# Two expert layers with a token mixer between them: gathered expert rows against both tables streamed through TensorE

## The reference, cut to what matters

```python
def peer_block(xb, w_q, sub_keys, expert_u, expert_v):
    q = (xb @ w_q).reshape(T, PEER_HEADS, 2, PEER_HALF)      # 8 heads
    s = einsum('thpd,hpkd->thpk', q, sub_keys)               # 2 x 128 keys
    sv, si = top_k(s, 16)
    cand = sv[:, :, 0, :, None] + sv[:, :, 1, None, :]
    cidx = si[:, :, 0, :, None] * 128 + si[:, :, 1, None, :]
    top_s, pos = top_k(cand, 16)
    eidx = take_along_axis(cidx, pos)                        # 16 experts a head
    gate = softmax(top_s)
    act = gelu(einsum('thkd,td->thk', expert_u[eidx], xb))
    return einsum('thk,thkd->td', gate * act, expert_v[eidx])
```

## Time and profile before

| | |
|---|---|
| time, median of 3 runs | 3167.44 us (3167.44 to 3170.0) |
| span of the profiled execution | 3165.3 us |
| TensorE busy | 2588.5 us (82%) |
| VectorE busy | 2022.9 us (64%) |
| ScalarE busy | 1229.5 us (39%) |
| bytes moved by DMA | 1179.94 MB, mean 373 GB/s |
| the indirect queue's packets | 82.1% of 16 DMA engines' span |

### The profile page before, as it was taken

One profiled execution on the slowest core, in us unless ns is written; L12 is line 12 of the kernel. 1 busy time (PEld: TensorE's weight loads), 2 busy tenths in 40 slices (PEclk: granted clock), 3 DMA queues, 4 the chain that ended last, 5 costly groups with the idle time before them and its releaser, 6 DMA issues.

```text
span 3165.3 us, 35978 instructions
## 1 busy us (share of the span) xinstructions
PE 2588.5 (82%) x12092; PEld 1064.0 (34%) x12092; DVE 2022.9 (64%) x5008; ACT 1229.5 (39%) x3892; POOL 1074.3 (34%) x1041
## 2 busy tenths in 40 slices
PE   7999998878777877778988878888777877978777
PEld 3555653323222323223333344333223332322111
DVE  4533457777777777665555757667777776765544
ACT  3122335443443444334323533444344543443323
POOL 0000014433433444333433334343443443343331
PEclk9999999899999989999999999999999999999999
DMA  9411359999999999999999999999999999999995
GB/s 353 155 54 53 125 204 405 421 421 418 415 420 421 419 408 414 418 417 411 418 415 417 416 411 393 416 419 421 420 418 417 416 419 416 405 420 422 418 421 243
DMA packets 198780, 1179.94 MB, mean 373 GB/s; under 512 B 20994, under 2 KB 21700, under 8 KB 67268
## 3 DMA queue, kind: packets, MB, share of 16 engines
q0 software_dynamic: 147456, 1073.81, 82.1%
q1 hardware_dynamic: 51140, 103.84, 8.9%
HBM read 1175.48 MB, written 2.10 MB: 372 GB/s over the span
## 4 chain that ended last, share of the span: by engine, by line
DMA 47%; PE 14%; ACT 5%; DVE 4%; issue 3%; POOL 3%; DVEq 0%; POOLq 0%
DMA ring<-in_expert_rows,idx_v 18%; DMA ring<-in_peer_rows,idx_v 11%; DMA scr<-in_expert_rows,idx_v 9%; DMA scr<-in_peer_rows,idx_v 8%; PE banks L1166 8%; PE banks L814 6%; DVE ring L2299 2%; POOL ring L788 1%; DVE scr L2299 1%; DMA scr<-in_w_in 1%; POOL scr L788 1%; ACT ring L1688 1%; ACT L1682 1%; ACT scr L1682 1%; ACT L1644 1%
## 5 line engine op out<-in xcount | busy, mean ns | idle before, releaser
L1166 PE MATMUL banks<-ring 128*32 128x512 f32 x2016 | 809.5, 621 | 251.7 <-ACT ring L1688 241.4
L1166 PE MATMUL banks<-scr,ring 128*32 128x512 f32 x2080 | 819.8, 613 | 215.5 <-ACT ring L1688 214.8
L1682 ACT ACTIVATE scr<-scr 128x1 f32<-128x1 f32 x1024 | 206.9, 202 | 1511.9 <-DVE scr L2299 1510.4
L2299 DVE CUSTOM_DVE_ANT_0 scr<-scr,ring 128x1024 f32<-128x1024 f32 x390 | 478.0, 1226 | 305.9 <-DMA scr<-in_peer_rows,idx_v 157.4
L2299 DVE CUSTOM_DVE_ANT_0 ring<-ring 128x1024 f32<-128x1024 f32 x378 | 463.1, 1225 | 302.0 <-DMA ring<-in_expert_rows,idx_v 166.7
L788 POOL DMA_INDIRECT scr<-in_peer_rows,idx_v x264 | 272.7, 1033 | 475.9 <-PE banks L1166 355.7
L814 PE MATMUL banks<-hT,scr 128*128 128x128 f32 (+3 forms) x2576 | 367.7, 303 | 66.4 <-DVE ring L2281 47.3
L1166 PEld LDWEIGHTS banks<-ring 128*32 128x32 f32 x2016 | 162.8, 111 | 770.2 <-ACT ring L1688 486.8
L788 POOL DMA_INDIRECT ring<-in_expert_rows,idx_v x256 | 271.1, 1059 | 422.1 <-PE banks L1166 389.3
L1166 PEld LDWEIGHTS banks<-scr,ring 128*32 128x32 f32 x2080 | 165.9, 111 | 737.3 <-ACT ring L1688 458.4
L788 POOL DMA_INDIRECT ring<-in_peer_rows,idx_v x248 | 263.1, 1061 | 409.4 <-PE banks L1166 371.0
(11 more groups left out here) (255 smaller groups left out, 2247.4 us busy)
## 6 DMA issues: line engine op xcount, KB each, us to landing
scr<-in_w_in SPq DMA_DIRECT2D x8, 2048.0 KB, 28.4
scr<-in_w_mod SPq DMA_DIRECT2D x7, 2048.0 KB, 12.8
ring<-in_w_in SPq DMA_DIRECT2D x7, 2048.0 KB, 12.8
scr<-in_w_q SPq DMA_DIRECT2D x6, 2048.0 KB, 27.8
ring<-in_w_mod SPq DMA_DIRECT2D x5, 2048.0 KB, 13.2
scr<-in_peer_w_q SPq DMA_DIRECT2D x4, 2048.0 KB, 12.3
scr<-in_peer_rows,idx_v POOLq DMA_INDIRECT x264
ring<-in_w_out SPq DMA_DIRECT2D x2, 2048.0 KB, 7.8
```

The source lines that it names most:

```text
L1166: last = nc.tensor.matmul(psum[2 + c][32 * g:32 * g + 32, :], spread[:, i % 8, :], rows[slot_of(i)][:, D + c * CW:D + (c + 1) * CW], start ...
L1682: nc.scalar.activation(gelu[:, h, k:k + 1], dots[:, h, k:k + 1], ACT.Gelu if i < N_ROWS else ACT.Gelu_apprx_tanh).then_inc(gelu_done, 1)
L2299: V.tensor_tensor_reduce(u, u, xq[g], 1.0, 0.0, ALU.mult, ALU.add, dots[:, n % 2, k:k + 1]).then_inc(dotted, 1)
```

## The change

No row of an expert is gathered any more. Two token tiles (a pair, 256 tokens) are taken together, and for each pair both tables are read from end to end, in 64 steps of 256 experts (two chunks of 128), 1 MB of each table in a step:

- `dense_half`: all activations of a chunk, 8 products of 256 columns (experts x tokens), so 16 in a step. ScalarE takes the gelu of both chunks with one instruction (`gelu_step`).
- `table` builds the gates as a table of 128 x 128 numbers for each token: the 128 picks of a token are turned into two one-hot matrices on VectorE (`hot_quad`, the second one scaled with the gate), and TensorE multiplies them, one product of 128 columns for each token. ScalarE copies it out (`table_copy`), and it is stored to HBM and read back in chunks of 2 MB (`load_gates`).
- `weigh`: VectorE multiplies activations with gates, 512 numbers a partition in a step.
- `sum_half`: the weighted activations times the second table, 4 products of 512 columns for each chunk, so 8 in a step, summed in four PSUM banks over all 64 steps.

For the first pair of a layer the gates are not there yet when the activations are: `first_of` does its 64 dense steps with its own routing and tables beside them and stores the activations to HBM; `second_of` fetches them, weighs and sums, with routing and tables of the second pair beside; `both_of` does dense and sum steps of the second pair in turn. The mixer of the second block is now `mix_second`, between the layers and with nothing beside it; the last gate runs for all four tiles at the end. Query weights are loaded for each tile instead of once for a layer. The joined tables, the indirect DMAs, `dot`, `add_row`, `quad_rows`, `to_quads` and `pack` are gone.

```diff
-                nc.gpsimd.indirect_dma_start(rows[slot], None, table,
-                                             bass.IndirectOffsetOnAxis(idx_v[:, n % IDX_HEADS, col_of(k):col_of(k) + 1], 0)
-                                             ).then_inc(row_in[slot], 16)
...
-                for c in range(2):
-                    last = nc.tensor.matmul(psum[2 + c][32 * g:32 * g + 32, :], spread[:, i % 8, :],
-                                            rows[slot_of(i)][:, D + c * CW:D + (c + 1) * CW],
-                                            start=(at_tile < 2), stop=(at_tile >= TILE_PAIRS - 2))
...
-                V.tensor_tensor_reduce(u, u, xq[g], 1.0, 0.0, ALU.mult, ALU.add, dots[:, n % 2, k:k + 1]).then_inc(dotted, 1)
...
+            def load_down(s):
+
+                if s >= 3:
+                    sp.wait_ge(dense_done, s - 2)
+                sp.dma_start(down_slot[s % 3], a[f"down{s // (2 * STEPS)}"][s % STEPS]).then_inc(down_in[s % 3], 16)
+
+            def load_up(u):
+
+                if u >= 3:
+                    sp.wait_ge(summed, u - 2)
+                sp.dma_start(up_slot[u % 3], a[f"up{u // (2 * STEPS)}"][u % STEPS]).then_inc(up_in[u % 3], 16)
...
+            def load_gates(pair, c):
+
+                n = CHUNKS_G * pair + c
+                if n >= 2:
+                    sp.wait_ge(gated, 8 * (n - 1))
...
+                sp.dma_start(gates[n % 2], gate_store[pair][:, :, c * P:(c + 1) * P].rearrange("g p x -> p g x")
+                             ).then_inc(gates_in[n % 2], 16)
...
+                for j in range(QUAD):
+                    last = mm(o[:, j * P:(j + 1) * P], hot_one[q % 2][:, j, :], hot_two[q % 2][:, j, :], 0, 1)
+                last.then_inc(table_done, 1)
...
+            def dense_half(s, c):
...
+                if c == 0:
+                    pe.wait_ge(down_in[s % 3], 16 * (s // 3 + 1))
+                    if s >= 2:
+                        pe.wait_ge(gelu_done, s - 1)
+                o = psum[4 + s % 2][:, c * PAIR:(c + 1) * PAIR]
+                for k in range(KT):
+                    last = mm(o, down_slot[s % 3][:, c, k, :], hT[:, k, tokens], k, KT)
...
+            def sum_half(u, c, first):
...
+                    pe.wait_ge(up_in[u % 3], 16 * (u // 3 + 1))
+                    pe.wait_ge(gated, u + 1)
+                w = act_half(u, first)[:, c * PAIR:(c + 1) * PAIR]
+                for side in range(2):
+                    for half in range(2):
+                        last = nc.tensor.matmul(psum[2 * side + half][:, :], w[:, side * P:(side + 1) * P],
+                                                up_slot[u % 3][:, c, half * CW:(half + 1) * CW],
+                                                start=(x == 0 and c == 0), stop=(x == STEPS - 1 and c == 1))
...
+            def both_of(pair):
+
+                pe.wait_ge(table_copied, 2 * TILE_QUADS * (pair + 1))
+                for x in range(2):
+                    for c in range(2):
+                        dense_half(STEPS * pair + x, c)
+                pe.wait_ge(x_added, 2 * pair)
+                for x in range(STEPS):
+                    for c in range(2):
+                        sum_half(STEPS * pair + x, c, 2 * BATCHES)
+                    if x + 2 < STEPS:
+                        for c in range(2):
+                            dense_half(STEPS * pair + x + 2, c)
...
+            def hot_quad(q):
...
+                V.tensor_tensor(hot_one[q % 2], iota.unsqueeze(1).to_broadcast([P, QUAD, P]),
+                                picks_t[:, 0, t0:t0 + QUAD].unsqueeze(2).to_broadcast([P, QUAD, P]), ALU.is_equal)
+                for j in range(QUAD):
+                    t = t0 + j
+                    last = V.tensor_scalar(hot_two[q % 2][:, j, :], iota, picks_t[:, 1, t:t + 1], picks_t[:, 2, t:t + 1],
+                                           ALU.is_equal, ALU.mult)
+                last.then_inc(hot_set, 1)
```

More of the change, by code:

```diff
@@ L178, in chunk_number, with spills_upto, fetches_upto @@
+def spills_upto(layer, r):
+    return layer * len(range(r % 3, BATCHES, 3)) + r // 3 + 1
+def fetches_upto(layer, r):
+    first = next(k for k in range(BATCHES, BATCHES + 3) if k % 3 == r % 3)
+    return layer * len(range(first, 2 * BATCHES, 3)) + (r - first) // 3 + 1
 def chunk_number(name, col=0):
@@ new lines, in second_of @@
+            def second_of(pair):
+                layer = pair // 2
+                load_gates(pair, 0)
+                for r in range(BATCHES, BATCHES + 3):
+                    fetch_acts(layer, r)
+                load_gates(pair, 1)
+                for x in range(STEPS):
+                    load_up(STEPS * pair + x + 3)
+                    if x % 2 == 1 and x // 2 + 3 < BATCHES:
+                        fetch_acts(layer, BATCHES + x // 2 + 3)
+                    if x % 8 == 7 and x // 8 + 2 < CHUNKS_G:
+                        load_gates(pair, x // 8 + 2)
@@ new lines, in _ @@
+            second_of(0)
+            both_of(1)
+            mix_second()
+            for n in range(2):
+                scores_q(N_HEADS + n)
+                scores_s(N_HEADS + n)
+            pe.wait_ge(x_added, TT)
+            first_of(2)
+            second_of(2)
+            both_of(3)
+            pe.wait_ge(x_added, 2 * TT)
+            pe.wait_ge(s_copied, ALL_HEADS)
+            for t in range(TT):
+                tile_rows("gp", t)
+                for n in range(2):
+                    gate(t, n)
+                products(t)
@@ new lines, in first_of, with second_of @@
+            def first_of(pair):
+                for x in range(STEPS):
+                    gelu_step(STEPS * pair + x, 0)
+                    beside_step(pair, x)
+                    if x in (STEPS - 4, STEPS - 2):
+                        q_out(PAIR_HEADS * (pair + 1) + (x - STEPS + 4) // 2)
+                    if x in (STEPS - 3, STEPS - 1):
+                        s_out(PAIR_HEADS * (pair + 1) + (x - STEPS + 3) // 2)
+            def second_of(pair):
+                for x in range(STEPS):
+                    beside_step(pair + 1, x)
@@ new lines, in _ @@
+            both_of(1)
+            mix_second()
+            for n in range(2):
+                q_out(N_HEADS + n)
+                s_out(N_HEADS + n)
+            first_of(2)
+            second_of(2)
+            both_of(3)
+            for t in range(TT):
+                act.wait_ge(x_added, TT + t + 1)
+                tile_square("gp", t)
+            for t in range(TT):
+                tile_root("gp", t)
+            for t in range(TT):
+                tile_out("gp", t, ple_gain, no_shift)
@@ new lines, in first_of, with second_of @@
+            def first_of(pair):
+                for x in range(STEPS):
+                    beside_step(pair, x)
+            def second_of(pair):
+                weigh(STEPS * pair, BATCHES)
+                weigh(STEPS * pair + 1, BATCHES)
+                for x in range(STEPS):
+                    if x + 2 < STEPS:
+                        weigh(STEPS * pair + x + 2, BATCHES)
+                    beside_step(pair + 1, x)
+                add_output(2 * (pair % 4))
+                add_output(2 * (pair % 4) + 1)
@@ L2367, in mid_final, with both_of @@
+            def both_of(pair):
+                for x in range(STEPS):
+                    weigh(STEPS * pair + x, 2 * BATCHES)
+                add_output(2 * pair)
+                add_output(2 * pair + 1)
+            in_gain, in_shift = (lambda k: gain[:, 2, k:k + 1]), (lambda k: mod[:, 3 * KT + k, 0:1])
+            mix_gain = lambda k: col("g_mix_2", k)
+            ffn_gain = lambda k: col("g_ffn_2", k)
+            ple_gain = lambda k: col("g_ple_2", k)
             def mid_final(t):
@@ new lines, in _ @@
+            add_projection(0, "wo", 0)
+            tile_stats("n1", 0)
+            tile_out("n1", 0, in_gain, in_shift)
+            for t in (1, 2, 3):
+                add_projection(0, "wo", t)
+                tile_stats("n1", t)
+            first_of(0)
+            second_of(0)
+            both_of(1)
+            mix_second()
+            first_of(2)
+            second_of(2)
+            both_of(3)
+            for t in range(TT):
+                tile_mean("gp", t)
+            for t in range(3):
+                tile_rstd("gp", t)
```

1171 lines of the change are left out of this document (484 added, 687 removed).

## The result

The changed kernel takes 4879.83 us (median of 4 runs, 4872.67 to 4880.86), the kernel before 3168.16 us beside it (3167.44 to 3170.0). The ratio is 1.5394, interval 1.5372 to 1.5416: 54% slower. The profiled execution has a span of 4878.1 us, 1.7 us under the median. The forecast was 4908 us, 0.6% above, and the range 4850 to 5060 holds the time.

The account below looks back on a forecast made before the run. It took the kernel before as DMA-bound and the changed one as TensorE-bound: opening 471, layers 4004, seams 46 and 6, mixer 272, tail 107 make 4906 us, plus 2.1 for the median 4908; range 4850 to 5060.

Parts of the forecast that it names:

- The price from a row of the opening: TensorE float32 products, start to start at full clock: 0.858 us for 512 columns, 0.431 for 256, 0.226 for 128.
- No wait in the steps: Dense and sum steps: TensorE never waits; dense step 6.9 us or more, sum 6.9, VectorE at most 5 us a step.
- The seams: Between first_of and second_of, each layer: gate chunk, fetches, landing, weighing 20 us plus 3 low clock; two seams 46 us.
- The missed wait: From second_of to both_of: two dense steps of 13.8 us cover the gate load but for 3 us, twice, 6 us.
- The mixer: Between the layers, all on TensorE's path: products 191 us, gaps 81 (between 40 and 150), together 272 us.
- The entry: Mixer gap at its start: two additions, four squares twice and two roots, 22 us.
- The late columns: Mixer gap: late columns behind loads landing after 13 to 28 us and behind VectorE's late pool, 25 us.
- Opening: Start of the kernel, unchanged up to the output projection at 393.75 us; first dense step at 471 us.
- Tail: End of the kernel: last gate of four tiles 76 us, entry 9, exit and final normalisation 22, together 107 us.
- A: Rival: in second_of gate chunks hold up table loads, TensorE waits 9 to 20 us 12 times, 5015 to 5150; chance 0.13.
- C: Rival: gate chunks at the seams go by bytes and the mixer's gaps are 40 us, 4840 us; chance 0.07.
- B: Rival: full products overlap like narrow ones, 0.12 us a record, 2782 us; deciding point 0.218 us a record; chance 0.01.

## Why the prediction was right

**The sign and the size of it.** The step that decided was to price the new products on TensorE and to find 3756 us of them, more than the whole kernel before. The two experiments that take half of a kind away gave back 811 and 809 us, and in *both_of* all but 1 to 9 us of 220 a stage. Products in bfloat16, at 3.8 times less each, brought the kernel from 54% slower to 5.5% faster. So the price of a product is the cause of the result.

**The price from a row of the opening.** 0.858, 0.431 and 0.226 us were read as starts to starts at full clock. The new stages came at 0.858 and 0.431. *second_of*, forecast 555, took 555.9 and 556.1; *both_of* of the first layer, 884 with its 3 us of wait, took 881.7. The mean of 594 or 379 ns that the groups show would have given a wrong sum, since records overlap.

**No wait in the steps.** The bounds for VectorE and ScalarE held: of theirs only 2.1 us, two waits on one-hots (L2216), show in the steps. One bound was wrong. ScalarE's table copies were put at no more than 693 ns, from a VectorE operation of the same number of elements; they took 1117. It did no harm with ScalarE 16% busy; in the kernels with products in bfloat16, where *first_of* is shorter by 220 us, it did.

**The seams.** Forecast 46 us with the low clock, measured 16.34 and 16.37 us of wait and 2.3 and 2.6 us of low clock, 37.6 together. TensorE at the first one:

```profile
1061.14 9.34 PE L1233 MATMUL banks<-ring,scr 128*128 128x512 f32 x16 [16.34 <-DVE scr L2232]
...
1073.90 7.03 PE L1233 MATMUL banks<-ring,scr 128*128 128x512 f32 x16
```

The mechanism was right: the gate chunk on SyncE's queue, fetches behind it, landing, weighing. SyncE's queue at this seam, and the weighing on VectorE:

```profile
1045.45 0.64 SPq L688 DMA_DIRECT2D scr<-gate_store  x1
1046.19 10.10 SPq L678 DMA_DIRECT2D scr<-act_store  x3
```
```profile
1060.30 1.96 DVE L2232 TENSOR_TENSOR scr<-scr 128x512 f32<-128x512 f32 x3 [33.81 <-DMA scr<-act_store]
```

The chunk's own issue takes 0.64 us; the hold shows at the fetches behind it. From the chunk to the next chunk, at 1056.34, are 10.9 us with three fetches in it, where 12.7 were put for the chunk alone; landing takes 4 more. So the price by piece was too high, the price by byte (3.2) too low. DMA's share is 1.07 at 319 GB/s from 1045 to 1061.1, so no run tells whether the pieces on the queue or the engines behind it set this time.

**The missed wait.** From *second_of* to *both_of* 3 us were forecast twice. The first layer had none, the second 15.5 and 1.6 of low clock. The step that failed is the statement that two dense steps cover the load: on SyncE's queue three loads for the last gate stand before these gate chunks in the second layer, and they were not counted there. They are in the changed code in plain sight. The term was 3 us and measured 17.1; the experiment that moves them gave 17.2 back. The 20.36 us that the two gate chunks take there is no price of theirs: with the three loads moved, the same two issues take 9.31 us.

**The mixer.** Forecast 272, measured 243, the largest error of the sum. Products and low clock were near: TensorE is busy 204.87 us for 191 at full clock, so at most 14 us of low clock for 18 forecast. The gaps were not: 243.0 - 204.87 = 38 us for the 63 forecast without the clock. The longest ones in TensorE's timeline of the mixer:

```profile
2514.13 6.48 PE L875 MATMUL banks<-scr,X 128*128 128x128 f32 x32 [15.44 <-DVE scr L1851]
...
2630.91 2.47 PE L875 MATMUL banks<-scr,X 128*128 128x128 f32 x16 [2.91 <-DVE scr L1851]
...
2686.53 2.18 PE L875 MATMUL banks<-hT,const 128*128 128x136 f32 x8 [7.79 <-DVE hT L2395]
```

The entry (22 forecast) is 15.44 and three small ones of 2.2 us in all. The late columns behind their loads (25) are 7.79 and 1.07: the weights `in_w_in` landed in 9.0 us at the median, with DMA's share at 0.27 in this stretch, and not in the 28.4 us of the earlier trace rows. The four chains of normalisation (16) are 2.9 and 2.7 and less. Each gap was bounded from a row where it stood alone; in the timeline most of these chains run beside groups of 14 us of another tile's products.

**The rest.** Opening 476.3 for 471: an extra idle of 4.17 us before the first queries, and those at half of the clock (6.52 us for 3.73). Tail 99.4 for 107: gaps of 20 us for 31. The errors: +5.3 opening, -4.1 and -7.0 *first_of* with its seam, +2.0 *second_of*, -2.3 and +14.9 *both_of*, -29 mixer, -7.6 tail, together -28. So a part of the closeness is luck: 22 us under-counted against 50 over-counted. The sum of bytes is off by a little too: its terms add up to 890 MB and not 888, and 891.28 were measured.

**The rivals.** A falls: no wait for a table in the changed kernel, and 10 us with twice the bytes. C, seams and mixer cheaper, was nearer in the mixer (40 us of gaps, the low clock among them, where at most 38 + 14 = 52 were measured and 81 forecast) and named the seams' sign; the time lies between C's 4840 and the forecast. B falls for float32, at 0.429 us a record; the bfloat16 kernels, at 0.225 us a product where B's point is 0.436, lie on its other side. The point itself was not measured. On the rule of the Trainium skill that stood beside B ("TensorE: Matmul & The Clock Gate", section "Back-to-back issue gap", 131 ns for a product of 512 columns in a stream): no trace here agrees. The shortest full product of 512 columns that these runs show is a bfloat16 one, 225 ns.

**What the new profile was to show.** TensorE 97% busy (over 90% asked), 4732.5 us for some 4650, 891.28 MB for 888, 183 GB/s for 180, a step of 13.77 us for 13.8, seams of 16 for 20.

## What to carry to other kernels

A change that takes bytes from DMA and gives work to TensorE is decided by one multiplication, products times their price from start to start in a row of the same shape and type, and that multiplication comes before any look at what is hidden; if it is longer than the kernel, no order of the code helps. The lever is then the price of a product (its type), not the order, and after that the next resource must be priced in its turn, as ScalarE's bfloat16 writes with a step showed. For waits, list all that stands on a DMA queue ahead of the load in question at each place where it is issued, also what only one of the passes has.

## What the runs showed of the hardware that was not expected

- A bfloat16 view of float32 data with a step of two elements, in both operands, costs TensorE next to nothing: 0.113 us for a product of 256 columns and 0.225 for 512 at full clock. Contiguous bfloat16 products of 128 columns, in the kernel with bfloat16 one-hots, take 0.22 us for four (609.82 - 609.60), 0.055 each, about the same for a column.
- Quarter products (32 columns of weights) go at 0.110 us a record, and four of them cost 2% more than the full one (7.01 us a step for 6.87). A change between narrow and full products costs some 0.2 us more: the dense step behind takes 7.10 us for 6.90.
- ScalarE's copy of 512 numbers from PSUM depends on the target: 1117 ns in float32 and 2638 ns in bfloat16 with a step of eight elements, while the gelu of 512 numbers, without a step, takes 600 ns in bfloat16 and 597 in float32. VectorE's weighing of 512 numbers went from 687 to 421 ns with bfloat16.
- After 16.34 and 16.37 us of idle TensorE's next 16 records took 9.34 and 9.59 us where 7.03 are usual, and 8.62 after 15.50: 2.3, 2.6 and 1.6 us of low clock, with a granted clock of 0.75, 0.73 and 0.82 over these stretches.

The rows of the third point: gelu, table copy and weighing of the changed kernel, and under them the weighing with bfloat16 activations and gates (groups as above).

```profile
L2232 DVE TENSOR_TENSOR scr<-scr 128x512 f32<-128x512 f32 x256 | 175.4, 687 | 1741.2 <-ACT scr L1668 1626.3
L1668 ACT ACTIVATE scr<-banks 128x512 f32<-128x512 f32 x256 | 152.8, 597 | 2399.6 <-PE banks L875 2399.6
...
L1659 ACT ACTIVATE scr<-banks 128x512 f32<-128x512 f32 x256 | 270.3, 1117 | 403.2 <-PE banks L875 403.2
```
```profile
L2242 DVE TENSOR_TENSOR scr<-scr 128x512 bf16<-128x512 bf16 x256 | 106.9, 421 | 701.3 <-ACT scr L1678 618.2 <-DMA scr<-act_store 59.7 <-DMA scr<-gate_store 23.4
```
